# Layer norms of a four-layer transformer kernel: modulation sums moved out of the first output phase, wide constant products in TensorE's pauses, two tiles centred before the scale

## What is computed

```python
for i in range(DEPTH):                      # DEPTH = 2
    ada = cs @ w_ada[i] + b_ada[i]          # modulation: 6 vectors of 1024 values
    sh1, sc1, g1, sh2, sc2, g2 = split(ada, 6)
    u = x * (1 + sc1) + sh1
    y = mixer(u)                            # layer 0: mLSTM, layer 1: differential attention
    x = layer_norm(ALPHA * x + (1 + g1) * y)
    u = x * (1 + sc2) + sh2
    y = conv_ffn(u)
    x = layer_norm(ALPHA * x + (1 + g2) * y)

def layer_norm(x, g, b):
    mu = mean(x); var = mean((x - mu) ** 2)
    return (x - mu) * rsqrt(var + 1e-5) * g + b
```

## Time and profile before

| | us |
|---|---|
| time, median of 3 runs | 2936.73 |
| the profiled execution's own time | 2937.88 |
| its span, first to last instruction | 2936.1 |
| mean granted TensorE clock | 0.979 of full |
| TensorE (matmul) busy | 2797.1 |
| VectorE busy | 1593.2 |
| ScalarE busy | 1046.6 |
| GpSimd busy | 1093.2 |

### The profile page before, as it was taken

The page is one execution under the profiler, slowest core; times in us unless marked ns, Lnnn a source line. Parts: engine busy times, 40 slices in busy tenths (PEclk is TensorE's granted clock), DMA queues, the critical chain, the costliest instruction groups (busy, mean ns, idle before and its releaser), DMA issues.

```text
span 2936.1 us, 37960 instructions
## 1 busy us (share of the span) xinstructions
PE 2797.1 (95%) x13936; PEld 2391.5 (81%) x13936; DVE 1593.2 (54%) x2341; ACT 1046.6 (36%) x1689; POOL 1093.2 (37%) x510
## 2 busy tenths in 40 slices
PE   4998899999899899999999999999999999999998
PEld 3885788887776678887897999999997977778887
DVE  6536766966555669986522423755553487332111
ACT  3333353423465443324311232222223338443222
POOL 2440254444422254445531333323335233334443
PEclk9999899999999899999899999999999999999999
DMA  5351345553321145554111122333332122122232
GB/s 214 112 186 44 108 139 197 186 189 126 131 84 61 51 141 193 188 186 136 44 61 56 50 87 79 129 129 129 116 128 79 58 90 66 62 86 93 97 97 86
DMA packets 89955, 329.83 MB, mean 112 GB/s; under 512 B 9956, under 2 KB 10724, under 8 KB 89320
## 3 DMA queue, kind: packets, MB, share of 16 engines
q1 hardware_dynamic: 85392, 312.21, 30.6%
q10 hardware_dynamic: 4440, 16.00, 1.6%
HBM read 324.50 MB, written 2.10 MB: 111 GB/s over the span
## 4 chain that ended last, share of the span: by engine, by line
PE 58%; DVE 2%; POOL 1%; ACT 1%; issue 1%; DVEq 0%; ACTq 0%; POOLq 0%
PE pair L1505 26%; PE pair L1507 18%; PE bank L1507 4%; PE pair L1347 1%; PE bank L1300 1%; PE pair L1363 1%; PE bank L1380 1%; PE bank L1347 1%; PE bank L1437 0%; PE pair L1461 0%; PE pair L1320 0%; PE bank L1320 0%; POOL UF L534 0%; PE bank L1287 0%; POOL UF L538 0%
## 5 line engine op out<-in xcount | busy, mean ns | idle before, releaser
L552 POOL TENSOR_TENSOR WL<-RAW,WH 128x1024 fp32r<-128x1024 f32 x392 | 983.4, 2510 | 1679.0 <-ACT WH L859 1065.3
L859 ACT ACTIVATE WH<-RAW 128x1024 fp32r<-128x1024 f32 x276 | 290.3, 1052 | 351.3 <-PE pair L1505 181.5
L1637 DVE CUSTOM_DVE_ANT_0 ADA<-ADA,CB 128x1024 f32<-128x1024 f32 x128 | 237.7, 1863 | 117.2 <-DMA ADA<-in_ast 105.9
L1770 DVE SCALAR_TENSOR_TENSOR XT<-pair,GATE,XT 128x512 f32 (+1 forms) x96 | 72.0, 750 | 348.0 <-PE pair L1507 179.7
L1505 PE MATMUL pair<-Uh,WH 128*128 128x384 f32 x832 | 214.0, 338 | 2.1 <-issue 2.1
L1505 PE MATMUL pair<-Ul,WH 128*128 128x384 f32 x832 | 211.1, 334 | 0.0
L1505 PE MATMUL pair<-Uh,WL 128*128 128x384 f32 x832 | 211.1, 334 | 0.0
L1507 PE MATMUL bank<-U1h,WH 128*128 128x512 f32 x480 | 187.2, 390 | 0.0
L1507 PE MATMUL bank<-U1h,WL 128*128 128x512 f32 x480 | 186.8, 389 | 0.0
L1507 PE MATMUL bank<-U1l,WH 128*128 128x512 f32 x480 | 186.8, 389 | 0.0
L1507 PE MATMUL pair<-U1h,WH 128*128 128x512 f32 x448 | 175.5, 392 | 2.8 <-POOL WL L552 2.8
(11 more groups left out here) (416 smaller groups left out, 6170.7 us busy)
## 6 DMA issues: line engine op xcount, KB each, us to landing
RAW<-in_wst SPq DMA_DIRECT2D x392, 512.0 KB, 3.5
ADA<-in_ast SPq DMA_DIRECT2D x192, 512.0 KB, 4.5
NB<-in_nbias ACTq DMA_DIRECT2D x8, 768.0 KB, 4.2
XT<-in_xt SPq DMA_DIRECT2D x1, 2048.0 KB, 15.4
STRIP<-in_strip ACTq DMA_DIRECT2D x8, 256.0 KB, 2.7
CB<-in_cb ACTq DMA_DIRECT2D x4, 512.0 KB, 4.1
DX<-in_dx ACTq DMA_DIRECT2D x1, 2048.0 KB, 8.0
out_xt<-XT SPq DMA_DIRECT2D x1, 2048.0 KB, 6.2
```

The source lines that it names most:

```text
L552: pool.tensor_tensor(WL[:, s4], RAW[:, s2], WH[:, s4].bitcast(F32), ALU.subtract)\
L859: act.activation(WH[:, c % 4], RAW[:, c % 2], ACT.Copy).then_inc(S("hi_done"), 1)
L1637: dve.tensor_tensor_reduce(tile, tile, cb[:, 0], 1.0, 0.0, ALU.mult, ALU.add, AD[:, u, 0:1])\
L1770: ins = dve.scalar_tensor_tensor(out=flat(XT[:, ds(jl, 1)]), in0=bank[:], scalar=gate_of(jl), in1=flat(XT[:, ds(jl, 1)]), op0=ALU.mult, op ...
```

## The change

Five edits.

1. The plan gives the modulation tiles 16 to 23 to jobs 8 to 15 of `qk`, 24 to 31 to `v`, 32 to 39 to `gate_o`, and none to `res` of layer 0.
2. The four constant matrices become parts of one buffer `STEADY` (512 columns), and `steady(n)` puts n wide products `MEAN`·`STEADY` into bank 0, whose result nobody reads. In `ln_pe` there are two ahead of the sums (behind a wait for the last reader of bank 0), one ahead of the wait for `ZS`, and in norms 0 to 2 one behind the wide mean, ahead of the spread of the scale, and two behind it.
3. DVE centres two tiles ahead of the scale, and tile t+2 behind the scaling of tile t.
4. `values_pe` starts a tile with the eight products of the four banks that need only its high part, and waits for the low part ahead of the other four; in both halves the order of the products is the new one.
5. `LN_END` gives each norm the end of its phase, for the wait of edit 2.

```diff
--- before.py
+++ after.py
@@ -62,7 +62,7 @@
 
 
 
-ADA_GROUPS = {40: (2, 4), 80: (0, 2), 96: (2, 4), 136: (0, 2)}
+ADA_GROUPS = {16: (2, 4), 40: (2, 4), 80: (0, 2), 96: (2, 4), 136: (0, 2)}
 
 
 def plan():
@@ -81,10 +81,10 @@
             adas.append(ada + 4 * (groups[1] - groups[0]))
 
 
-    add("qk", 16, 0, "u", 0)
-    add("v", 8, 0, "u", 0, ada=16)
-    add("gate_o", 8, 0, "u", 0, ada=24)
-    add("res", 8, 0, "o", 0, gate=2, ada=32)
+    add("qk", 16, 0, "u", 0, ada=16)
+    add("v", 8, 0, "u", 0, ada=24)
+    add("gate_o", 8, 0, "u", 0, ada=32)
+    add("res", 8, 0, "o", 0, gate=2)
 
     def ffn(layer, u_fill, h_fill, ada):
         for g in range(3):
@@ -256,10 +256,8 @@
         OH = at("OH", [KT, T], A_B, F32R)
         OL = at("OL", [KT, T], A_B + 16 * KB, F32R)
         o = A_C
-        IDENT = at("IDENT", [P], o); o += 512
-        MEAN = at("MEAN", [P], o); o += 512
-        HALF = at("HALF", [P], o); o += 512
-        TRI = at("TRI", [P], o); o += 512
+        STEADY = at("STEADY", [T], o); o += 4 * T
+        IDENT, MEAN, HALF, TRI = (STEADY[:, m * P:(m + 1) * P] for m in range(4))
         PRM = at("PRM", [NPRM], o); o += (4 * NPRM + 31) // 32 * 32
         MOD = at("MOD", [NADA, 2], o); o += 8 * NADA
         AD = at("AD", [4, 2], o); o += 32
@@ -442,6 +440,9 @@
 
             what = norm_after(p)
             return what[1] if what and what[0] == "ln" else None
+
+
+        LN_END = {ends_in_ln(p): p["j0"] + p["n"] for p in PHASES if ends_in_ln(p) is not None}
 
         def ln_slots(idx, u):
 
@@ -1172,15 +1173,16 @@
                 pe.wait_ge(S("lo_done"), p["j0"] + j + 1)
                 for kk in range(2):
                     k = 2 * i + kk
-                    if half == 0:
-                        pe.wait_ge(S("u_ready"), p["fill"] + k + 1)
-                    for b in range(4):
-                        if half == 1 and k == 0 and b >= 2:
-                            pe.wait_ge(S("bank_read"), p["j0"] + b - 1)
-                        for m, (x, w) in enumerate(((U1h, WH), (U1l, WH), (U1h, WL))):
-                            mm = pe.matmul(BANK[VT_BANKS[half][b]][:], x[:, k, b * P:(b + 1) * P],
-                                           flat(w[:, i, 4 * kk:4 * kk + 4]),
-                                           start=k == 0 and m == 0, stop=k == KT - 1 and m == 2)
+                    for m, parts in enumerate((((U1h, WH), (U1h, WL)), ((U1l, WH),))):
+                        if half == 0:
+                            pe.wait_ge(S("u_ready" if m else "u_hi"), p["fill"] + k + 1)
+                        for b in range(4):
+                            if half == 1 and k == 0 and b >= 2 and m == 0:
+                                pe.wait_ge(S("bank_read"), p["j0"] + b - 1)
+                            for x, w in parts:
+                                mm = pe.matmul(BANK[VT_BANKS[half][b]][:], x[:, k, b * P:(b + 1) * P],
+                                               flat(w[:, i, 4 * kk:4 * kk + 4]),
+                                               start=k == 0 and m == 0 and w is WH, stop=k == KT - 1 and m == 1)
                 mm.then_inc(S("pe_job"), 1)
 
         def diff_pe(pe):
@@ -1536,12 +1538,21 @@
                 pe.wait_ge(S("ctx_scale"), k + 1)
                 widen(BANK[7], 60, 2, "ctx_wide")
 
+            def steady(n):
+
+                for _ in range(n):
+                    pe.matmul(BANK[0][:], MEAN[:], STEADY[:], start=True, stop=True)
+
             def ln_pe(idx):
+
                 by_token, rest = (BANK[b] for b in LN_BANKS[idx][2:])
+                pe.wait_ge(S("bank_read"), LN_END[idx] - 3)
+                steady(2)
                 pe.wait_ge(S("sq_add"), 5 * idx + 5)
                 token_sums(by_token, 0, SQ[:, 0], True, False)
                 pe.wait_ge(S("squared"), 8 * idx + 7)
                 token_sums(by_token, 0, SQ[:, 6], False, False)
+                steady(1)
                 pe.wait_ge(S("z_sum"), 2 * idx + 2)
                 token_sums(BANK[1], 0, ZS[:, 0:T], True, True).then_inc(S("d_sum"), 1)
                 pe.wait_ge(S("squared"), 8 * idx + 8)
@@ -1550,7 +1561,11 @@
                 if idx == 3:
                     pe.wait_ge(S("dve_squares"), 1)
                     token_sums(BANK[3], 0, CSQ[:], True, True).then_inc(S("cs_sum"), 1)
+                else:
+                    steady(1)
                 widen_tokens(idx + 1)
+                if idx != 3:
+                    steady(2)
 
             def rms_pe(k, ctx):
                 pe.wait_ge(S("x_sum"), 8 * k)
@@ -1954,14 +1969,14 @@
                 dve.wait_ge(S("token_root"), idx + 1)
                 dve.reciprocal(SM[:, 56:60], SM[:, 48:52]).then_inc(S("token_scale"), 1)
                 dve.wait_ge(S("mean_sum"), 2 * idx + 2)
-                for t in range(4):
+                for t in range(2):
                     centre(t)
                 dve.wait_ge(S("scale_wide"), idx + 1)
                 for t in range(KT):
                     dve.wait_ge(S("centred"), 8 * idx + t + 1)
                     dve.tensor_tensor(XT[:, t], XT[:, t], BANK[2][:], ALU.mult).then_inc(S("normed"), 1)
-                    if t + 4 < KT:
-                        centre(t + 4)
+                    if t + 2 < KT:
+                        centre(t + 2)
                     if idx != 3 and t >= 1:
                         lo_one(UFILL[idx], t - 1)
                     if idx == 3 and t == 6:
```

## The result

| | before | after |
|---|---|---|
| time, median | 2935.57 us (20 runs, 2932.96 to 2941.17) | 2942.88 us (20 runs, 2939.21 to 2945.05) |
| span of the profiled execution | 2936.1 | 2942.4 |
| mean granted clock | 0.979 | 0.981 |

The change makes the kernel slower: the ratio after/before is 1.0022, 95% interval 1.0015 to 1.0029, and the medians differ by 7.3 us. The forecast was 2935.8 with a range of 2929 to 2942. The time lies outside the range, though the difference from before is under the 0.3% that the chances went by.

The account below looks back on a forecast made before the run. TensorE, busy 95% of the span, was taken as the bound, so only its waits could pay. Terms summed to -0.9 us: 2937.88 became 2937.0, and with the profiled execution 1.15 above the median, 2935.8; range 2929 to 2942.

Parts of the forecast that it names:

- Part 1: Modulation tiles moved from res to qk: norm 0's ZS at about 343.8, not 350.8; qk costs 0 (0 to +3).
- Rival D: In qk, modulation products over 2.8 us make ACT round late and TensorE wait: up to +3, 2938.8 us; chance 0.08.
- full-clock end: Norm 0's bound if the clock stays full: scale spread at 349.9, term -8.0 us.
- half-clock end: Norm 2's bound if the added products run at half clock: term +3.5 us.
- Part 3: Two tiles centred ahead in the norms: ACT ends 0.75 us later behind the first scaled tile; worth nothing alone.
- part 2: Constant products ahead of the norms' sums and scale: their added time is given back only if the clock stays full.
- Part 4: values_pe's earlier start in vt only lengthens the 2.52 us wait for ACT's copies; +0.6 us taken.
- rival C: In vt the copies hang on TensorE, so the earlier start carries: -5.2 us, 2931.5 us; chance 0.12.
- A: Clock held in all norms but norm 2: -7.6 us, 2929.1 us; chance 0.14.
- B: Constant products in the norms run at half clock and everything behind waits: +7.0 us, 2943.8 us; chance 0.10.

Follow-up runs that it names:

- best4: Changed kernel with convolution ahead of the modulation product in qk, no constant products, old order in values_pe, four tiles centred ahead; 2928.37 us, ratio to before 0.9967.
- four_centred: Changed kernel with four tiles centred ahead of the scale instead of two; 2938.03 us, ratio to before 1.0008.
- no_ada: Changed kernel with the modulation tiles put back where they were before; 2945.61 us, ratio to before 1.0027.
- best: Changed kernel with convolution ahead of the modulation product in qk, no constant products, old order in values_pe, two tiles centred ahead; 2929.60 us, ratio to before 0.9977.
- experiment 5: Changed kernel with the order of products in values_pe as before; last product of vt 2.84 us earlier, time 2941.50 us.
- no_products: Changed kernel without the constant products, their wait and the order around them kept; 2937.97 us, ratio to before 1.0002.
- old_values: Changed kernel with the order of products in values_pe as before; 2941.50 us, ratio to before 1.0020.
- conv_first: Changed kernel with a job's convolution ahead of its modulation product in qk; 2936.07 us, ratio to before 0.9994.
- ada_only: Kernel before with only the modulation tiles moved; 2935.73 us, ratio to before 0.9986.

## Why the prediction was wrong, point by point

| term | predicted (bounds) | measured, after less before |
|---|---|---|
| `qk` | 0 (0 to +3) | +7.4 |
| mLSTM core and `res` | none | -3.0 |
| norm 0 | -6.5 (-8.0 to -3.9) | -8.6 |
| norm 1, to ACT's end | +1.9 (-0.15 to +4.0) | +2.9 |
| `vt` behind it | +0.6 (0.45 to 0.85) | +2.2 |
| norm 2 | +2.2 (-3.2 to +3.5) | +3.2 |
| norm 3 | +0.9 (-1.2 to +2.6) | +1.6 |
| all behind | none | +0.5 |
| sum | -0.9 | +6.2 |

- **`qk`, the step that failed.** Part 1 counted VectorE's work in a job (4.9 to 6.9 us in 5.44), asked whether VectorE falls behind, and for the loads said that they go with the weight loads "with the same slack". VectorE never was short of time: all its products in `qk` but the first (1.88) took 1.22 to 1.33 us, the low end. The slack was not the same, since in `qk` ACT's rounding stands behind the job's output work, and this now stood behind a load. Rounding makes `WL`, and `WL` releases the next load: a ring of 13.65 us for two jobs. Its pieces could be read from the trace of before (the product's 1.22, the load, the convolution, Silu, rounding, `WL`), but their sum was not made. Rival D priced the same place by VectorE's slowness, a condition that didn't come about, and at 3 us.
- **mLSTM core.** In before the clock is at half for 6.8 us behind the start of this stage, in after for 3.4, which is worth 1.7 of the 2.5. This share is luck of the execution: `best4`, with no modulation tiles in `res`, has the long low stretch too (62.64 us), and of the two traces of `four_centred` one has the short one (61.00) and the other the long one (62.22). The rest goes with the move of the modulation tiles: at the start of the core TensorE waits for the load of `SEL`, 3.40 us in before and 3.41 in `no_ada`, and 2.25 to 2.64 in all kernels with the tiles moved. `res` itself is 0.5 shorter without the tiles. The prediction had none of the three.
- **Norm 0** was right in mechanism, and the clock held, so that it came out at its full-clock end (-8.0) and a little beyond. But the products have little part in it: with the tiles moved alone it is -7.2.
- **Norms 1 and 2** were right in mechanism (products at half clock on the path), and the values taken, between two levels of the clock, were each 1.0 too low. Norm 2 lies near its half-clock end, norm 1 between the two.
- **Norm 3** was off by 0.7, and its mechanism was wrong: the added products ran at full clock, and the first scaled tile came 0.4 earlier. The +1.6 is made of these -0.4, of +1.17 from centring (0.6 predicted), and of +0.8 at the start of the next phase, whose first products run at half clock for 5.8 us, a term that the prediction did not have. In the second trace of the changed kernel this norm lost nothing (46.55 against 46.65).
- **Part 3** was right in its price: ACT ends 0.72 us later behind the first scaled tile (0.75 predicted). It was wrong in that the part is worth nothing. That holds where the scale comes in time (`best` and `best4`), but not beside the constant products of part 2, which hold the scale back at half clock: there four centred tiles are 4.9 us faster, of which norm 2 shows 0.7 and the rest is not divided.
- **Part 4** was right in that the early start is lost in the wait for the copies, and rival C fell: the wait grew from 2.5 to 3.2 and a second one of 3.6 came ahead of it. The term was mis-sized, 0.6 against 2.2. In the term are 0.2 and 0.9 (a longer step of POOL, below) ahead of the restart and 1.05 behind it. What the prediction left out is the clock behind a longer pause; experiment 5 puts the edit at 2.8.
- **The rivals.** A (the clock is held) came true in norm 0, and in norm 3 up to the wide mean. B's time, 2943.8, is 0.9 from the measured one, but that is luck: its mechanism carried only norms 1 and 2. Norm 0 went against it, and the 7.4 us of the ring stand in for that.
- **A reading of the rows.** The prediction put the `ZS` row (7.6 us in 3 waits) on the layer norms. Those three waits are the second block's; in norms 0, 1 and 3 the pause ahead of the `ZS` sums is 2.21, 0.75 and 0.75 us. No term of the sum used the 7.6.
- **What would show it.** The text named "if TensorE waits in `qk`" as a sign of being wrong. It waited one phase later, in `v`, as three jobs of lead took the first of it.

## What to carry to other kernels

When a load is given to a phase, don't only ask whether some engine has the time. Follow who waits behind the instruction that waits for the load, and whether that chain comes back to the issue of the next load; then add up the ring and compare it with the bound engine's time for as many jobs as there are loads under way (here 13.65 us against 10.88 for two). If the ring is longer, put the work that releases weights ahead of the work that waits for the load; here that one change of order was worth 7 us. Work that is put into a pause to hold the clock costs its half-clock time if it stands ahead of something on the path and the clock falls all the same: here it gave 0.8 us in one norm and cost 2.5 and 3.1 in two others.

## What the runs showed of the hardware

- The clock fell in norm 1 of the changed kernel though TensorE had no pause there that the trace shows; it was doing single-column sums and a few wide float32 products (busy 3.00 of 3.00 us at 0.50 right behind the fall). In the same stretch of `four_centred` one execution had a clock of 1.00 and another 0.59. The difference between these two was 2.3 us at the first scaled tile. A comparison of two single traces in a stage with light TensorE work can be off by that much.
- A modulation product of VectorE and GpSimd's work hold each other up. In before the product takes 1.21 to 1.23 us in all 118 cases in which it starts with GpSimd idle, and up to 6.00 us (median 2.65) in the 74 in which it starts while GpSimd works.
- Behind norm 1 this decides which of the two is late. The last of POOL's eight gain steps takes 1.73 to 1.75 us and not 0.77 in six of the kernels (eight traces): the changed one, `no_ada`, `no_products`, `four_centred`, `old_values` and `conv_first`. In all eight the modulation product starts 0.2 to 0.5 us ahead of that step. In the other four traces (before, `ada_only`, `best`, `best4`) it starts 0.3 to 1.1 us behind the start of that step, which then takes 0.76 to 0.78, and the product takes 5.5 to 6.2 us. Here the changed kernel and then `ada_only`; POOL's eight steps are one row:

```profile
752.90 6.99 POOL L525 TENSOR_SCALAR XT<-XT,PRM 128x512 f32<-128x512 f32 x8
757.62 1.63 DVE L1652 CUSTOM_DVE_ANT_0 ADA<-ADA,CB 128x1024 f32<-128x1024 f32 x1 [6.96 <-DMA ADA<-in_ast]
```

```profile
749.95 6.03 POOL L524 TENSOR_SCALAR XT<-XT,PRM 128x512 f32<-128x512 f32 x8
756.14 5.63 DVE L1637 CUSTOM_DVE_ANT_0 ADA<-ADA,CB 128x1024 f32<-128x1024 f32 x1 [8.41 <-DMA ADA<-in_ast]
```

The product starts when its tile has landed, 4.3 to 4.6 us behind the issue in the eight traces and 5.2 to 5.9 in the four. In these four, and in no other, a 16 KB packet of the instruction queue moves during that load:

```profile
q8 instruction: 1, 0.02, 0.9%
```

(`ada_only`, window 750 to 757 us; the same window of the changed kernel's load, 753 to 758, has no such row.) So the 1 us on the path of `vt` goes with where a load of instructions falls. No run moved that load by itself, so this is what all twelve traces have in common, not a cause that was tested.
